# Three small edits ahead of the expert stage: first loads of x split finer, two projections given banks of their own, an earlier request for spread rows

## The reference

```python
q, fr, iv, g, z, xbc, dt, gate_a, gate_b = split(x @ w_in)       # one wide projection
o, s_hg_new = hgrn2_recurrence(silu(q), k, v, log_f, s_hg)        # chunks of 32
out_a = (rms_norm(o) * sigmoid(g)) @ hg_proj
xbc, conv_new = causal_dwconv(xbc, conv_prev, conv_w, conv_b)     # width 4, then silu
y, h_new = ssd_recurrence(xs, dt, a, bm, cm, h_ssm)               # Mamba-2 state space
out_b = (rms_norm((y + d_skip * xs) * silu(z))) @ ssd_proj
h = layer_norm(ALPHA * x + (sigmoid(gate_a) * out_a + sigmoid(gate_b) * out_b) @ w_out)
x = layer_norm(ALPHA * h + moe_ffn(h))                            # top 4 of 32 experts
```

## Time and profile before

| | us |
|---|---|
| time, median of 3 runs (lowest, highest) | 1507.08 (1507.07, 1507.94) |
| the profiled execution's own time | 1507.74 |
| its span | 1506.0 |
| PE busy | 1466.5 (97%) |
| DVE, ACT, POOL busy | 446.8, 344.6, 107.3 |
| moved from and to device memory | 507.75 MB, mean 337 GB/s |

### The profile page before, as it was taken

One profiled execution on the slowest core, in us unless ns is written; L12 is line 12 of the kernel. 1 busy time (PEld: TensorE's weight loads), 2 busy tenths in 40 slices (PEclk: granted clock), 3 DMA queues, 4 the chain that ended last, 5 costly groups with the idle time before them and its releaser, 6 DMA issues.

```text
span 1506.0 us, 21874 instructions
## 1 busy us (share of the span) xinstructions
PE 1466.5 (97%) x8606; PEld 733.3 (49%) x8606; DVE 446.8 (30%) x918; ACT 344.6 (23%) x863; POOL 107.3 (7%) x95
## 2 busy tenths in 40 slices
PE   9999999999999999999999999999999999999997
PEld 7777776566777764333333333333333333333332
DVE  3653777867410137201101111111111101101113
ACT  1224215631110023211212112122112111211213
POOL 1002231010502401000000000000000000000000
PEclk9999999999999999999999999999999999999999
DMA  6346697546269777999999999999999999999996
GB/s 214 112 168 176 214 292 228 184 153 197 93 213 297 289 278 281 421 418 429 427 427 428 429 429 429 427 429 427 429 428 429 428 429 429 428 429 428 430 427 262
DMA packets 110574, 507.75 MB, mean 337 GB/s; under 512 B 12548, under 2 KB 49012, under 8 KB 85844
## 3 DMA queue, kind: packets, MB, share of 16 engines
q1 hardware_dynamic: 103840, 499.64, 83.0%
q10 hardware_dynamic: 6676, 7.29, 1.7%
HBM read 491.19 MB, written 15.72 MB: 337 GB/s over the span
## 4 chain that ended last, share of the span: by engine, by line
PE 67%; DMA 21%; DVE 3%; ACT 1%; issue 1%; DVEq 0%; SPq 0%; ACTq 0%
DMA wGU<-in_w_gu 21%; PE ps L2483 16%; PE ps L1944 12%; PE ps L2488 8%; PE ps L2251 4%; PE ps L2424 4%; PE ps L1960 3%; PE ps L2471 3%; PE ps L2475 3%; PE ps L2268 2%; PE ps L2389 2%; PE ps L2281 2%; PE ps L2405 1%; DVE up L1837 1%; DVE up L1836 1%; PE ps L2026 1%
## 5 line engine op out<-in xcount | busy, mean ns | idle before, releaser
L2483 PE MATMUL ps<-wGU,xe 128*64 128x512 f32 x1536 | 343.7, 595 | 15.6 <-DMA wGU<-in_w_gu 15.6
L2488 PE MATMUL ps<-wD,aT 128*64 128x512 f32 x1024 | 226.8, 595 | 0.0
L2483 PEld LDWEIGHTS ps<-wGU,xe 128*64 128x64 f32 x1536 | 108.5, 137 | 238.0 <-issue 211.3
L1944 PE MATMUL ps<-xT,ring 128*128 128x288 f32 (+1 forms) x848 | 180.7, 410 | 2.2 <-PEq L200 0.7
L1833 DVE TENSOR_SCALAR sg<-sg 128x512 f32<-128x512 f32 x32 | 13.7, 427 | 558.3 <-ACT sg L1276 558.3
L1944 PEld LDWEIGHTS ps<-xT,ring 128*128 128x128 f32 (+1 forms) x848 | 126.5, 172 | 46.3 <-issue 4.4
L2488 PEld LDWEIGHTS ps<-wD,aT 128*64 128x64 f32 x1024 | 71.4, 137 | 133.0 <-issue 126.2
L1276 ACT ACTIVATE sg<-ps 128x512 f32<-128x512 f32 x32 | 19.1, 598 | 487.3 <-PE ps L2471 487.3
L1225 ACT ACTIVATE xe<-ps,lnT 128x64 f32<-128x64 f32 x262 | 81.4, 422 | 1.2 <-PE ps L2398 1.2
L402 PE MATMUL ps<-xT,ring 128*128 128x288 f32 x320 | 78.1, 407 | 0.0
L1292 ACT COPY ysb<-ps 64x512 f32<-64x512 f32 x64 | 37.1, 580 | 155.3 <-PE ps L2488 154.5
(11 more groups left out here) (487 smaller groups left out, 1418.9 us busy)
## 6 DMA issues: line engine op xcount, KB each, us to landing
wGU<-in_w_gu SPq DMA_DIRECT2D x128, 2048.0 KB, 34.9
wD<-in_w_down SPq DMA_DIRECT2D x64, 2048.0 KB, 36.1
ring<-in_w_in SPq DMA_DIRECT2D x21, 2048.0 KB, 8.9
out<-hst SPq DMA_DIRECT2D x8, 1024.0 KB, 6.0
ringS<-in_ssd_proj SPq DMA_DIRECT2D x4, 2048.0 KB, 8.9
wbuf<-prompt_A_rows ACTq DMA_DIRECT2D x16, 384.0 KB, 4.3
out<-Sb SPq DMA_DIRECT2D x2, 2048.0 KB
ring<-in_hg_proj SPq DMA_DIRECT2D x2, 2048.0 KB, 9.2
```

Source lines behind the costliest of these rows:

```text
L1944: last = m.matmul(ps[h, b, 0:T], ring[c % 2][:, k, n * P + h.start:n * P + h.stop], xT[:, k, :], start=(k == 0), stop=(k == KD - 1))
L2483: last = m.matmul(ps[half[h], bank, :], xe[:, f, hx, :], wgu[n][:, k, col + CW * h:col + CW * h + CW], start=(i == 0 and k == 0), stop=False)
L2488: last = m.matmul(ps[half[h], B_Y, :], aT[:, k, i - 4, :], wdn[n][:, k, CW * h:CW * h + CW], start=False, stop=(i == 5 and k == 3))
```

## The change

- x comes in three column parts: 0:256, 256:512 and 512:1024. SP issues tile 0 of the first part, then the first two rows of the weight chunk as pieces of 256 KB each, then part two of x (three transfers), weight rows 2:4, part three of x (three), weight rows 4:6 and 6:8. ACT issues tile 1 and the sample tile of the first part. ACT's small loads wait for the third part.
- The dummy products are eight instead of twelve. Two blocks of x are turned before the first product instead of three; the other six follow inside the k loop.
- `project(1)` writes bank 3 and `project(I_Q + 1)` bank 6; `bank_free` waits for the last projection that used the same bank. The scores of group 3, which use bank 3, wait for `q_zc` 2.
- The doubled sum is formed once; the sum over the samples moves one step up and to columns 128:160.
- `spread(0)` and `spread(1)` are issued by ACT after `evacuate(I_Z + 13)`, in the seventh sample's turn, no longer after `evacuate(I_Z + 14)` and behind the load of `ws`. The load of `ws` stays there.

```diff
-        s_in = [S1(f"x_columns_loaded{i}") for i in range(2)]
+        s_in = [S1(f"x_columns_loaded{i}") for i in range(3)]
...
-                sp.dma_start(xtok[:, 0, 0:CW], x_prompt[0, 0:P, 0:CW]).then_inc(s_in[0], 16)
-                sp.dma_start(xtok[0:32, 2, 0:CW], x_s[:, 0:CW]).then_inc(s_in[0], 16)
-                for i in range(4):
-                    if i == 1:
-                        for t in range(2):
-                            sp.dma_start(xtok[:, t, CW:D], x_prompt[0, P * t:P * t + P, CW:D]).then_inc(s_in[1], 16)
-                        sp.dma_start(xtok[0:32, 2, CW:D], x_s[:, CW:D]).then_inc(s_in[1], 16)
-                    sp.dma_start(ring[0][:, 2 * i:2 * i + 2, :], w_k[:, 2 * i:2 * i + 2, C_X:C_X + CW]).then_inc(s_first[i] if i < 3 else s_w[0], 16)
+                sp.dma_start(xtok[:, 0, 0:256], x_prompt[0, 0:P, 0:256]).then_inc(s_in[0], 16)
+                for k in range(2):
+                    sp.dma_start(ring[0][:, k:k + 1, :], w_k[:, k:k + 1, C_X:C_X + CW]).then_inc(s_first[k], 16)
+                for j, cols in ((1, slice(256, CW)), (2, slice(CW, D))):
+                    for t in range(2):
+                        sp.dma_start(xtok[:, t, cols], x_prompt[0, P * t:P * t + P, cols]).then_inc(s_in[j], 16)
+                    sp.dma_start(xtok[0:32, 2, cols], x_s[:, cols]).then_inc(s_in[j], 16)
+                    sp.dma_start(ring[0][:, 2 * j:2 * j + 2, :], w_k[:, 2 * j:2 * j + 2, C_X:C_X + CW]).then_inc(s_first[1 + j], 16)
+                sp.dma_start(ring[0][:, 6:8, :], w_k[:, 6:8, C_X:C_X + CW]).then_inc(s_w[0], 16)
...
-                act.dma_start(xtok[:, 1, 0:CW], x_prompt[0, P:2 * P, 0:CW]).then_inc(s_in[0], 16)
-                act.wait_ge(s_in[1], 48)
+                act.dma_start(xtok[:, 1, 0:256], x_prompt[0, P:2 * P, 0:256]).then_inc(s_in[0], 16)
+                act.dma_start(xtok[0:32, 2, 0:256], x_sample.rearrange("b s d -> (b s) d")[:, 0:256]).then_inc(s_in[0], 16)
+                act.wait_ge(s_in[2], 48)
...
-                for _ in range(12):
+                for _ in range(8):
...
-                    if k % 4 == 0:
-                        pe.wait_ge(s_in[k // 4], 48)
+                    if k in (0, 2, 4):
+                        pe.wait_ge(s_in[k // 2], 48)
...
-                for k in range(3):
+                for k in range(2):
                     turn(k)
...
-                    if k + 3 < KD:
-                        turn(k + 3)
+                    if k + 2 < KD:
+                        turn(k + 2)
...
         def z_bank(i):
 
+            if i == 1:
+                return 3
+            if i == I_Q + 1:
+                return 6
...
                     if b == NB - 1:
+                        act.wait_ge(q_h[2], 64)
+                        act.dma_start(ws[0:32].rearrange("p h t -> p (h t)"), rows_s.rearrange("h t -> (h t)").partition_broadcast(32)).then_inc(r_aw, 16)
+                    evacuate(I_Z + 2 * b + 1)
+                    if b == NB - 2:
                         act.wait_ge(r_aw, 1 + 48)
                         act.wait_ge(q_h[1], 64)
-                        act.wait_ge(q_h[2], 64)
-                        act.dma_start(ws[0:32].rearrange("p h t -> p (h t)"), rows_s.rearrange("h t -> (h t)").partition_broadcast(32)).then_inc(r_aw, 16)
                         spread(0)
                         spread(1)
-                    evacuate(I_Z + 2 * b + 1)
...
-                        if i > 0:
-                            pe.wait_ge(q_zc, i - 1 if z_bank(i) == 0 or z_bank(i - 1) == 0 else i)
+                        before = [j for j in range(i) if z_bank(j) == z_bank(i)]
+                        if before:
+                            pe.wait_ge(q_zc, before[-1] + 1)
...
-                    if k in (4, 5):
-                        c = 32 * k - 32
-                        m.matmul(ps[:, 4, c:c + 32], ones[:], d0, start=True, stop=False)
-                        m.matmul(ps[:, 4, c:c + 32], ones[:], d1, start=False, stop=True)
-                    if k == 6:
-                        m.matmul(ps[0:32, 4, 160:192], sbatch[:], d2, start=True, stop=True)
+                    if k == 4:
+                        m.matmul(ps[:, 4, 96:128], ones[:], d0, start=True, stop=False)
+                        m.matmul(ps[:, 4, 96:128], ones[:], d1, start=False, stop=True)
+                    if k == 5:
+                        m.matmul(ps[0:32, 4, 128:160], sbatch[:], d2, start=True, stop=True)
...
                 for g in range(SG):
+                    if g == 3:
+                        pe.wait_ge(q_zc, 2)
```

More of the change, by code:

```diff
@@ L186, in build @@
         s_ones = S1("ones_ready")
-        s_first = [S1(f"first_chunk_loaded{i}") for i in range(3)]
+        s_first = [S1(f"first_chunk_loaded{i}") for i in range(4)]
         s_dtq = S1("dt_quarters_ready")
@@ L384, in _ @@
                     pe.wait_ge(s_xte, k + 1)
-                    if k % 2 == 0:
-                        pe.wait_ge(s_first[k // 2] if k < 6 else s_w[0], 16)
+                    if k < 2 or k % 2 == 0:
+                        pe.wait_ge((s_first[0], s_first[1], s_first[2], None, s_first[3], None, s_w[0])[k], 16)
                     for mt in range(4):
@@ L1352, in _ @@
                 for t, (_, rows) in enumerate(TILES):
-                    last = v.tensor_tensor(dtmp[0:rows, t, :], ps[0:rows, 4, 96 + 32 * t:128 + 32 * t], av[0:rows, t, :], ALU.subtract)
+                    last = v.tensor_tensor(dtmp[0:rows, t, :], ps[0:rows, 4, 96 + 16 * t:128 + 16 * t] if t != 1 else ps[:, 4, 96:128], av[0:rows, t, :], ALU.subtract)
                 last.then_inc(q_dif, 1)
```

## The result

The changed kernel takes 1524.05 us (median of 4 runs, 1522.98 to 1524.43), the kernel before 1507.51 in the same session (1507.07 to 1511.40). The ratio is 1.0104, 95% interval 1.0091 to 1.0116. I had forecast 1503.5, a range of 1502.7 to 1506.0, and a chance of 0.08 for slower. The time lies 18 us above the upper end of the range.

The account below looks back on a forecast made before the run. TensorE was taken to bound 67% of the chain, transfers 21% (expert stage, tied to TensorE's schedule). Terms 1.0 + 0.7 + 0.7 + 0.44 + 0.8 = 3.6 us off 1507.08 gave 1503.5, range 1502.7 to 1506.0.

Parts of the forecast that it names:

- The stop at 238.87: Inside project(I_Q): a stop without semaphore, read as waiting for an instruction packet, would go; 0.8 us saved, bounds 0 and 0.88.
- The first rival: The stop at 238.87 stays or comes at another place; sum 2.8 us, time 1504.2; chance 0.25.
- The clock: At the start, short stops keep TensorE at or return it to the lower clock; slower, such as 1511.2; chance 0.08.
- The beginning: Start to k loop's end: first product 1.55 us earlier at 6.05, 0.55 paid back; net 1.0, bounds -0.3 and 1.3.
- The banks and the sum: project(1) and project(I_Q + 1) run without waiting, 0.7 us each; doubled sum formed once saves 0.44 us.
- The spread rows: Before the first pair: earlier request keeps VectorE's work hidden, wins nothing directly; costs at worst 0.3 to 0.5 us.
- Whether it passes to the end: Savings before about 600 us reach the expert stage's end at full size; rival that they do not: 1507.0, chance 0.06.

Follow-up runs that it names:

- -8: Two projections in banks of their own and the doubled sum formed once, against the kernel before; 8 TensorE instructions fewer ahead of the loop; 1507.34 us, ratio 0.9994.
- +96: 24 tiny products (96 instructions) put in front of project(0) in the kernel before; 1508.92 us, ratio 1.0010.
- place 0: Same TensorE instruction count ahead of the loop as the kernel before, which took 1507.51 us in the changed kernel's session.
- +1: One instruction more ahead of the loop than the kernel before: changed kernel plus six tiny products, 1510.42 us; two versions with spread rows unmoved, 1505.27 and 1505.71.
- the version at +1 with 12 dummies: Changed kernel with spread rows asked for where they were, 12 dummies and two tiny products; 1505.71 us, ratio 0.9981 to the kernel before.

## Why the prediction was wrong

**The failed step: "counted in instructions" was worked out for one stop only.** Under "The stop at 238.87" I had the change's 24 instructions and the packets, and asked only what they do at that one stop. The same shift moves the loop of six blocks against the packets' edges. I never asked why no packet is fetched after 791: it is because the body is kept, and that hangs on where it lies. The first rival came nearest: it had the stop come at another place, but priced it at the 0.8 us of the stop, ahead of the loop, and had packets fetched all along, where the kernel before fetches none from 791.3 on. "The clock" was my only slower case. The measured price is 9 to 13 us by the loop's length in four kernels (11.6 in the changed one). It is less than the sum of the stops (30.1 us in the changed kernel) because TensorE's waits for weights (15.6 + 6.5 us at the gate/up lines before) vanish behind them: the chain that ended last went through the weights' transfers before, and goes through TensorE after.

The Trainium skill, in Runtime: NRT & Kernel Launch (Instruction fetch mechanics), says that instructions come in blocks of 16 KiB (256 instructions) into a memory that for TensorE holds 2048, refilled as a FIFO, and that a taken branch whose target isn't in the current window of two pages forces a fetch before work goes on. The traces agree on the blocks: 1.31 MB in 80 packets are 16 KB each, and the run with 232 more fits the period of 256. They do not agree with a window of two pages: the body has 1718 instructions by my count of the program, nearly seven blocks, and 13 kernels jump back over it without a fetch. By the size of 2048 it fits, but not much more beside it. That the first packet of the body is overwritten by one fetched ahead at its end is my reading and is not shown. In its plain form, with room for seven packets, it fails: a body of 1718 lies within seven at 75 places of 256, but it was kept at both -8 and +96, 104 apart.

**The beginning** (forecast 1.0 earlier, measured 1.25 later). The data were in time, as forecast: no wait, first product at 6.30 for 6.05. What failed is "the clock", kept at 0.08. Mean passes of the k loop's line: with 12 dummies 415 to 417 ns in eleven profiles; with 8 dummies 452, 450, 453, 460 and once 417; with 6 dummies 446. So fewer dummies put the rise behind the first product in five profiles of six. I had taken the moment of the rise (near 4.8) as fixed once TensorE works without a break. In the two versions that differ in this (and in the four tiny products that keep the place), the k loop ends at 25.91 with 12 dummies and 27.58 with 8, but their medians are equal (1506.72, 1506.71). The two executions that were profiled took 1505.88 and 1508.43, so the 1.7 us belong to single executions, and the medians don't show them. With 12 dummies, the x parts end the k loop at 25.49 to 26.90 (four profiles, mean 26.3) and without them at 25.91 to 27.14 (seven, mean 26.5): 0.2 us, inside their own spread, for my 1.0. With 8 dummies they count for more: 27.27 to 27.58 in three profiles, and 28.95 without the parts in one. And where the clock rose in time with 8 dummies, the first product came at 5.47 and the k loop ended at 24.64, 1.5 earlier than before. So the data side of the forecast was right; the clock took it back in three of the four profiles that have 8 dummies and the x parts.

The Trainium skill, in TensorE: Matmul & The Clock Gate (The HAM clock gate), which I had weighed as a budget of time, also says that the moment varies from run to run. These profiles agree: with 12 dummies alone they take from 4.33 to 5.49 us for 24 passes.

**The banks and the sum** (0.7 + 0.7 + 0.44): right. From the k loop's end to the scores the changed kernel gains 1.2 us on the one before (107.64 against 108.84), for 1.14; the passes of `project(I_Q)` and its neighbour run through in 7.98. In the changed kernel that second gain is lost again at the first pair.

**The stop at 238.87** (0.8): it is gone in the changed kernel. But my reason was only half right. It is there in the kernel before (place 0) and in one of the three versions at +1, and not in the other two, nor in the two other kernels at place 0. So the place alone does not fix that stop; what moves the fetch is open.

**The spread rows** ("at worst 0.3 to 0.5"): mis-sized by four times or more. I had named the mechanism (the 768 KB run beside the store, `ws` behind it) and guessed 1 to 2 us of delay. It was 3.3 for the store and 2.5 for `ws`, and VectorE's queue has the bound of `ws` ahead of the gathering, so everything for the first pair was late. Measured: 2.0 us in the kernel before, 5.6 with the banks freed. A part of the latter is the clock, the third rival at a place that it did not name: the wait of 3.6 us is followed by 13 us at a granted clock of 0.87.

**Whether it passes to the end.** Savings pass only in part: the version at +1 with 12 dummies enters the loop 2.8 us earlier and ends 2.0 earlier.

**The sum, put right** by the two traces' checkpoints: start +1.25, banks and sum -1.2, read-out and first pair +2.1, until the wait at 298 another +1.5 (the clock behind the first pair's wait), the stop at 333 +1.3, the loop +11.6: together 16.55, for the 16.5 between the ends.

## What to carry to other kernels

Before an edit that changes the number of instructions ahead of a long loop, look at the fetches of instructions over the loop: if they stop after the first turn, the body is kept, and a few instructions more or less may end that. A stop for "issue" at each turn, with more packets of instructions, is the sign, and a handful of tiny products, whose results nobody uses, is the test and in this kernel was the cure. Test more than one number of them: 24 instructions more helped the changed kernel, and 232 more harmed the kernel before. A request moved up costs what it shares the queues with: find the small transfer that someone waits for.

## What was not expected of the hardware

- A loop body of 1718 TensorE instructions was kept or fetched anew by a shift of 8 to 16: 42 against 80 packets, 9 to 13 us over five turns. In the changed kernel each return to the body's start had stops of about 2.3 and 4.1 to 4.7 us, and the granted clock around the first was 0.84 over 22 us.
- Behind the second stop 13 passes take 4.77 us, where 16 took 3.61: some of them go at the 1.2 GHz pace, though TensorE had stood only 2.4 and 4.1 us. One wait of 3.6 us at the first pair was followed by a granted clock of 0.88 over 12.5 us.
- Two requests of 384 KB each held up a running store by 3.3 us and a load of 128 KB behind it by 2.5; one of them held up the store by 1.5.
